# Stick-breaking suffix sums as products of rounded parts, in a two-layer encoder kernel

## The reference, cut to what matters

```python
z = q @ k^T * 64 ** -0.5                        # 8 heads, head width 64
strict = key_pos[None, :] < q_pos[:, None]
log_keep = where(strict, log_sigmoid(-z), 0.0)
later = cumsum(log_keep, axis=3, reverse=True) - log_keep
a = where(strict, exp(log_sigmoid(z) + later), 0.0)
o = a @ v
```

## Time and profile before

| what | value |
|---|---|
| median of 3 runs | 2169.91 us (2168.7 to 2170.88) |
| profiled execution, its time | 2169.05 us |
| its span in the trace | 2167.3 us |
| PE busy | 2155.3 us, 99% |
| PE weight loads busy | 1957.7 us, 90% |
| DVE busy | 1531.3 us, 71% |
| ACT busy | 1193.8 us, 55% |
| POOL busy | 706.7 us, 33% |

### The profile page before, as it was taken

One profiled execution on the slowest core, in us unless ns is written; L12 is line 12 of the kernel. 1 busy time (PEld: TensorE's weight loads), 2 busy tenths in 40 slices (PEclk: granted clock), 3 DMA queues, 4 the chain that ended last, 5 costly groups with the idle time before them and its releaser, 6 DMA issues.

```text
span 2167.3 us, 41214 instructions
## 1 busy us (share of the span) xinstructions
PE 2155.3 (99%) x14116; PEld 1957.7 (90%) x14116; DVE 1531.3 (71%) x2728; ACT 1193.8 (55%) x1956; POOL 706.7 (33%) x342
## 2 busy tenths in 40 slices
PE   8999999999999999999999999999999999999999
PEld 6789999999999988888877899999999999888887
DVE  5767857977777766666567678599777786666665
ACT  5755445478777533333367545454777785333332
POOL 1400006887777500000023000178777774000000
PEclk9999999999999999999999999999999999999999
DMA  6444564655555555555555445556555555655554
GB/s 230 152 146 139 177 186 143 184 176 165 164 158 162 175 194 193 193 194 193 194 191 155 145 149 185 157 160 185 173 161 164 161 160 178 192 193 193 193 194 155
DMA packets 103764, 377.26 MB, mean 174 GB/s; under 512 B 11760, under 2 KB 11760, under 8 KB 103152
## 3 DMA queue, kind: packets, MB, share of 16 engines
q1 hardware_dynamic: 102528, 371.24, 54.4%
q10 hardware_dynamic: 1136, 4.79, 0.6%
HBM read 374.94 MB, written 1.05 MB: 173 GB/s over the span
## 4 chain that ended last, share of the span: by engine, by line
PE 99%; DVE 1%; ACT 0%; DMA 0%; issue 0%; SPq 0%; ACTq 0%; DVEq 0%
PE ps L499 31%; PE ps L500 30%; PE ps L501 30%; PE ps L831 3%; PE ps L508 1%; PE ps L632 1%; PE ps L792 1%; PE ps L605 0%; PE ps L593 0%; PE ps L704 0%; PE ps L697 0%; DMA raw<-in_stream 0%; DVE hT_lo L1265 0%; PE ps L620 0%; DVE w_lo L1248 0%; PE ps L608 0%
## 5 line engine op out<-in xcount | busy, mean ns | idle before, releaser
L499 PE MATMUL ps<-hT_hi,w_hi 128*128 128x256 f32 x2688 | 765.6, 285 | 0.6 <-DVE hT_lo L1265 0.6
L1114 ACT ACTIVATE w_hi<-raw 128x1024 fp32r<-128x1024 f32 x512 | 523.3, 1054 | 438.3 <-PE ps L501 437.9
L500 PE MATMUL ps<-hT_lo,w_hi 128*128 128x256 f32 x2688 | 760.6, 283 | 0.0
L501 PE MATMUL ps<-hT_hi,w_lo 128*128 128x256 f32 x2688 | 760.5, 283 | 0.0
L484 POOL TENSOR_TENSOR w_lo<-raw,w_hi 128x1024 fp32r<-128x1024 f32 x264 | 633.9, 2416 | 271.3 <-ACT w_hi L1114 271.3
L499 PEld LDWEIGHTS ps<-hT_hi,w_hi 128*128 128x128 f32 x2688 | 515.8, 192 | 3.1 <-issue 3.0
L500 PEld LDWEIGHTS ps<-hT_lo,w_hi 128*128 128x128 f32 x2688 | 515.8, 192 | 0.1
L501 PEld LDWEIGHTS ps<-hT_hi,w_lo 128*128 128x128 f32 x2688 | 515.6, 192 | 0.0
L499 PE MATMUL ps<-w_hi,wgt_hi 128*128 128x512 f32 x1024 | 398.6, 389 | 0.0
L500 PE MATMUL ps<-w_lo,wgt_hi 128*128 128x512 f32 x1024 | 398.4, 389 | 0.0
L501 PE MATMUL ps<-w_hi,wgt_lo 128*128 128x512 f32 x1024 | 398.4, 389 | 0.0
(11 more groups left out here) (189 smaller groups left out, 2559.3 us busy)
## 6 DMA issues: line engine op xcount, KB each, us to landing
raw<-in_w_u SPq DMA_DIRECT2D x256, 512.0 KB, 3.6
raw<-in_w_v SPq DMA_DIRECT2D x256, 512.0 KB, 3.7
raw<-in_stream SPq DMA_DIRECT2D x192, 512.0 KB, 3.6
arena<-in_bias ACTq DMA_DIRECT2D x2, 1024.0 KB, 5.9
arena<-in_subk ACTq DMA_DIRECT2D x2, 1024.0 KB, 6.3
x<-in_x SPq DMA_DIRECT2D x4, 256.0 KB, 4.9
out<-x SPq DMA_DIRECT2D x4, 256.0 KB, 2.1
arena<-in_params ACTq DMA_DIRECT2D x2, 283.5 KB, 4.3
```

The source lines that it names most:

```text
L499: mm(out_, left[0], right[0], start=start, stop=False, skip_group_check=group)
L500: mm(out_, left[0], right[1], start=False, stop=False, skip_group_check=group)
L501: return mm(out_, left[1], right[0], start=False, stop=stop, skip_group_check=group)
L1114: f(w_hi[:, slot, :], raw[:, slot, :], ACT.Copy).then_inc(hi_ready.sem, 1)
```

## The change

Four things change.

`c_later` multiplies rounded parts instead of f32 numbers: `from_here` and `ones` are copied once per layer into `sums_r` (fp32r), `ce` is rounded into `keep_hi` by ACT and its rest is written into `keep_lo` by DVE. Each f32 product becomes two fp32r products.

ACT gets `round_keep(0)` in its table at 19 and `round_keep(1)` at 21. DVE gets `rest_keep(0)` at 20, between `c_keep(1)` and `c_take_later(0)`, and `rest_keep(1)` at 21, ahead of `c_take_later(1)`.

`c_later` waits on PE for `keep_split` (DVE's `rest_keep` done) in place of `masks_ready` and `keep_ready`.

`c_scores` does two calls at once, and its products alternate between the two row halves. It stands at slots 10, 11 and 13 instead of 10, 10, 11, 11, 12 and 13.

```diff
                 def c_scores(c):
 
+                    pe.wait_ge(side_ev.sem, side_ev.at(layer, max(4, c + 2)))
+                    kt, _, heads = c_heads(c)
+                    n = (2 - kt) * P
+                    for j in range(len(heads)):
+                        for d in range(2):
+                            h = c_heads(c + d)[2][j]
+                            rows = slice(64 * d, 64 * d + 64)
+                            last = mm(ps[:, 4 + (c + d) % 4, j * n:(j + 1) * n],
+                                      qkT[rows, 5, h // 2, kt * P:(kt + 1) * P], qkT[rows, 4, h // 2, kt * P:T],
+                                      start=True, stop=True)
+                            if j == len(heads) - 1:
+                                last.then_inc(side_mm.sem, 1)
...
-                    pe.wait_ge(masks_ready.sem, masks_ready.at(layer, 1))
-                    pe.wait_ge(keep_ready.sem, keep_ready.at(layer, 1 if c < 3 else 2))
+                    pe.wait_ge(keep_split.sem, keep_split.at(layer, 1 if c < 3 else 2))
                     if c >= 2:
                         pe.wait_ge(loga_ready.sem, loga_ready.at(layer, c - 1))
-                    last = mm(ps[:, 6 + c % 2, :], from_here, ce[:, c, :], start=True, stop=(kt == 1))
+                    mm(ps[:, 6 + c % 2, :], sums_r[:, 0, :], keep_hi[:, c, :], start=True, stop=False)
+                    last = mm(ps[:, 6 + c % 2, :], sums_r[:, 0, :], keep_lo[:, c, :], start=False, stop=(kt == 1))
                     if kt == 0:
                         g = (c - 2) // 2
-                        last = mm(ps[:, 6 + c % 2, :].rearrange("p (h q) -> p h q", h=2)[:, :, P:T], ones,
-                                  ce[:, par_, 2 * g * P:(2 * g + 2) * P].rearrange("p (h q) -> p h q", h=2),
-                                  start=False, stop=True)
+                        for part, keep_ in enumerate((keep_hi, keep_lo)):
+                            last = mm(ps[:, 6 + c % 2, :].rearrange("p (h q) -> p h q", h=2)[:, :, P:T], sums_r[:, 1, :],
+                                      keep_[:, par_, 2 * g * P:(2 * g + 2) * P].rearrange("p (h q) -> p h q", h=2),
+                                      start=False, stop=(part == 1))
...
-                    10: ((c_scores, 0), (c_scores, 1)), 11: ((c_scores, 2), (c_scores, 3)),
-                    12: ((c_scores, 4),), 13: ((c_scores, 5),),
+                    10: ((c_scores, 0),), 11: ((c_scores, 2),), 13: ((c_scores, 4),),
...
+                def round_keep(i):
+
+                    if i == 0:
+                        act.wait_ge(masks_ready.sem, masks_ready.at(layer, 1))
+                        f(sums_r[:], view(MASKS + P, 2, P), ACT.Copy)
+                    act.wait_ge(keep_ready.sem, keep_ready.at(layer, i + 1))
+                    f(keep_hi[:, 3 * i:3 * i + 3, :], ce[:, 3 * i:3 * i + 3, :], ACT.Copy).then_inc(keep_rounded.sem, 1)
...
-                    18: ((take_ab_transposes, 0),), 23: ((c_weights, 0), (take_ab_transposes, 1)),
+                    18: ((take_ab_transposes, 0),), 19: ((round_keep, 0),), 21: ((round_keep, 1),), 23: ((c_weights, 0), (take_ab_transposes, 1)),
...
+                def rest_keep(i):
+
+                    dve.wait_ge(keep_rounded.sem, keep_rounded.at(layer, i + 1))
+                    v.tensor_tensor(keep_lo[:, 3 * i:3 * i + 3, :], ce[:, 3 * i:3 * i + 3, :],
+                                    keep_hi[:, 3 * i:3 * i + 3, :].bitcast(F), ALU.subtract).then_inc(keep_split.sem, 1)
...
-                    19: ((c_sums, 1), (head_norm, 3)), 20: ((c_keep, 1), (c_take_later, 0)),
-                    21: ((c_take_later, 1), (head_block, 2)), 22: ((c_take_later, 2), (head_norm, 4)),
+                    19: ((c_sums, 1), (head_norm, 3)), 20: ((c_keep, 1), (rest_keep, 0), (c_take_later, 0)),
+                    21: ((rest_keep, 1), (c_take_later, 1), (head_block, 2)), 22: ((c_take_later, 2), (head_norm, 4)),
```

More of the change, by code:

```diff
@@ L160, in build @@
         y_parts = (y_a, y_b, y_c)
+        _, keep_hi, keep_lo = overlay(("at_gate", [P, GATE], F), ("keep_hi", [P, 6, 512], FR), ("keep_lo", [P, 6, 512], FR))
+        _, sums_r = overlay(("at_mrg", [P, MRG + 512], F), ("sums_r", [P, 2, P], FR))
         arena = sb("arena", [P, KEYS * T])
@@ L262, in build @@
         keep_ready = Signal(sem("keep_ready"), 2)
+        keep_rounded = Signal(sem("keep_rounded"), 2)
+        keep_split = Signal(sem("keep_split"), 2)
         later_mm = Signal(sem("later_mm"), 6)
@@ L586, in c_scores @@
                 def c_scores(c):
-                    kt, par_, heads = c_heads(c)
-                    pe.wait_ge(side_ev.sem, side_ev.at(layer, max(4, c + 1)))
+                    pe.wait_ge(side_ev.sem, side_ev.at(layer, max(4, c + 2)))
+                    kt, _, heads = c_heads(c)
                     n = (2 - kt) * P
[L591 to L595, removed]
@@ L596, in c_scores @@
-                    last.then_inc(side_mm.sem, 1)
+                    for j in range(len(heads)):
[7 more added lines that the diff above has]
+                                last.then_inc(side_mm.sem, 1)
```

## The result

The changed kernel takes 2179.44 us (median of 6 runs, 2178.61 to 2181.28) against 2169.23 us (2167.86 to 2170.88) of the kernel before: 10.2 us more, a ratio of 1.005, interval 1.004 to 1.006 (8.7 to 13 us). The forecast was 2180.5 us on a median of 2169.91, which is 10.6 us more. The profiled execution has 2178.69 us and a span of 2177.0.

A forecast was written before the change was run, and what follows sets the result against it. PE was taken as the bound throughout. Per layer -1.9 (scores) - 3.3 (suffix sums) + 8.1 (stall) + 2.4 (clock) = +5.3 us, +10.6 us in two layers, giving 2180.5 us on the median; range 2174.5 to 2186 us.

The forecast's parts named there:

- The scores: c_scores on PE: calls 4 and 5 together save 1.26 us, calls 0 and 1 some 0.6; 1.86 us per layer.
- The suffix sums: c_later on PE: fp32r pairs replace f32 products, 1.31 us becomes 0.69 in calls 2 to 5; saves 3.3 us per layer.
- The stall: PE at c_later(0) waits for keep_lo from rest_keep(0), behind c_keep(1) on DVE: 8.1 us per layer, twice.
- The clock: PE's products behind each stall run at half clock: 2.4 us lost per stall, bounds nothing and twice that.
- stall without clock loss: Rival: PE stalls but keeps full clock; +2.9 us per layer, 2175.8 us; chance 0.16.
- Behind the stall: DVE and ACT pieces after c_later(0)'s wait: delays are covered by slots in hand, costed at nothing.
- second wait: Rival: DVE pieces behind the stall reach PE too late; further 2 to 4 us per layer, some 2186 us; chance 0.14.
- The sum: Whole kernel: scores, suffix sums, stall and clock give +5.3 us per layer, +10.6 us in two, 2180.5 us; chance 0.64.

The follow-up runs named there:

- The scores alone: Kernel before with only the new c_scores and its new table, suffix sums as before: 2164.68 us against 2168.83, ratio 0.9981.
- the wait alone: Kernel before with c_later(0) to (2) waiting for c_keep(1) instead of c_keep(0), nothing else changed: 2186.84 us against 2168.83, ratio 1.008.
- the suffix sums alone: Changed kernel with the old c_scores and its old table: 2182.97 us against 2168.83 of the kernel before, ratio 1.0065.
- filling the wait: Changed kernel with 32 unused fp32r products on PE ahead of c_later(0)'s wait: 2175.88 us against 2168.83 of the kernel before, ratio 1.0031.
- early_filled: Changed kernel with rest_keep(0) ahead of c_sums(1) on DVE and 10 unused products before c_later(0)'s wait: 2170.26 us against 2168.69 of the kernel before.
- early_moved_filled: Changed kernel, rest_keep(0) ahead of c_sums(1), ab_transposes(2) and ACT's copy a slot later, 10 unused products in the wait: 2167.77 us against 2169.16 before.
- staggered: Changed kernel, rest_keep(0) ahead of c_sums(1), PE's c_later one slot later, transposes one or two, ACT's copies following: 2161.72 us against 2169.32 before.
- early_rest: Changed kernel with rest_keep(0) moved on DVE to right behind split(23), ahead of c_sums(1) and head_norm(3): 2168.51 us against 2169.32 of the kernel before.

## Why the prediction was right

**The scores.** Predicted 1.26 us for calls 4 and 5 in one and 0.6 us for calls 0 and 1; the rows give 1.26 and 1.84 - 1.30 = 0.54 us. That is 1.8 us per layer, 3.6 in all; predicted were 3.7. The scores alone gave 4.2 us, with an interval of 2.2 to 6.1.

**The suffix sums.** Predicted 0.69 us for a call with both kinds, measured 0.70.

**The stall.** Predicted 8.1 us twice, measured 16.2 us in two. The step that carried the forecast was to see where the awaited piece stands in DVE's order, not how long it is: the wait alone, with no work added, showed 6.4 of it. That both ends move together with the scores was shown by the suffix sums alone, which have the same 8.1 us.

**The clock.** Predicted 2.4 us per stall, from the span's start; 2.1 us by the steps in the timeline, 1.96 us by filling the wait. The rival "stall without clock loss" is out. The granted clock fell during the stall, and in another kernel it fell already during one of 2.5 us. The Trainium skill, page "TensorE: Matmul & The Clock Gate", section "Why this matters for your kernels", advises against gaps above about 3 us between bursts of matmuls. The long stall agrees; the one of 2.5 us was shorter than that and still did it.

That the size came out so near was partly luck. The start of the span is no fixed price: in the changed kernel's profile full speed is back there earlier than before:

```profile
10.02 0.77 PE L504 MATMUL ps<-w_hi,hT_hi 128*128 128x512 f32 x1 [1.25 <-DVE hT_lo L1281]
...
12.72 0.51 PE L504 MATMUL ps<-w_hi,hT_hi 128*128 128x512 f32 x1
13.06 0.39 PE L505 MATMUL ps<-w_lo,hT_hi 128*128 128x512 f32 x1
...
14.58 0.48 PE L504 MATMUL ps<-w_hi,hT_hi 128*128 128x512 f32 x1
```

Seven products take 13.06 - 10.02 = 3.04 us, 1.45 us more than at full speed. Read from this start, the forecast would have had some 1.5 us in place of 2.4.

**Behind the stall.** No second wait of PE came in the changed kernel. That was argued from PE's later needs, and the changed profile lists none; DVE waits for PE instead, 1.32 us ahead of `c_take_later(0)`, as predicted. How thin the cover is shows where the stall is gone: head_norm(5) and `c_take_later(3)` were the next to come late, 0.35 to 1.9 us.

**The sum.** Per layer: -1.8 - 3.3 + 8.1 + 2.1 = +5.1 us, twice 10.2 us, and the medians have 10.2. That they agree to the tenth is chance: the interval is 8.7 to 13 us. The two profiles, compared product by product in PE's order, give it more closely. The product at 42.82 us of the trace before is 1.3 us early in the changed kernel, the one at 105.82 is 4.0 us late: 5.3 us in the first layer. In the second it is 4.45 us late at 1117.20 and 9.7 at 1181.62, 5.2 us. The span grew by 9.7 us and not by 10.5, because the changed kernel's profiled execution gained 1.3 us at its start (15.89 - 14.58), as shown above, and lost 0.5 us in small steps elsewhere.

## What to carry to other kernels

With engines that run in program order, price a new wait by the place of the awaited instruction in its engine's queue. Here a piece of 1.7 us, put behind a late one, cost a stall of 8.1, and moving that one piece took 5.6 us of it away. When PE is the bound, look at which piece comes late next before you count a gain: twice here (`early_filled`, `early_moved_filled`) the next one took the gain. And count the clock with the stall, but only where PE is what the stretch waits for afterwards.

## What the runs showed of the hardware

A wait of PE of 2.5 us halved the clock for the next 3 us of products (granted 0.50 from 82.10 to 85.20); in `early_filled` one of 1.9 us did the same. In `staggered`, waits of 0.95 us left no slow step behind them, nor did waits of 1.4 us in `early_moved_filled`. The end of the trace before already pointed there, with the clock down some 2 us after PE's last work, but the expectation for `early_rest` made nothing of it.

A plain f32 product of 512 columns costs 0.88 us here and its two-part fp32r form 0.45; with 256 columns the pair of them costs 0.24 us against 0.43 (1.31 - 0.88). So rounding into two parts about halves the cost on PE where, as with the ones of these two matrices, one operand needs no second part.

Products on the two row halves ran side by side also when four records of one half stood ahead of the other's: eight records in 1.14 us, four in 1.13. With eight records of one half ahead they did so only in part: 1.84 us in that order, 1.30 us alternating.
